# A split-precision SwiGLU layer on one core: both token halves share each weight tile, the gate-up product goes through memory, and the down projection sums over all channels in PSUM

## The reference, cut to what matters

```python
def _rmsnorm(x, g):
    xf = x.astype(jnp.float32)
    y = xf * lax.rsqrt(jnp.mean(xf * xf, axis=-1, keepdims=True) + EPS)
    return (y * g.astype(jnp.float32)).astype(x.dtype)
    ...
    h = _rmsnorm(x, g_fp)
    f = (jax.nn.silu(h @ w_g) * (h @ w_u)) @ w_d
    x = x + _rmsnorm(f, g_fq)
```

## Time and profile before

| | us |
|---|---|
| median of 3 runs | 1560.63 (1560.19 to 1563.69) |
| the profiled execution | 1561.2 |
| its span, first to last instruction | 1559.3 |
| PE busy | 1494.7 (96%) |
| DVE busy | 958.9 (61%) |
| ACT busy | 683.7 (44%) |
| POOL busy | 460.6 (30%) |
| TensorE clock granted, mean | 0.991 |

### The profile page before, as it was taken

The page is one execution under the profiler, slowest core; times in us unless marked ns, Lnnn a source line. Parts: engine busy times, 40 slices in busy tenths (PEclk is TensorE's granted clock), DMA queues, the critical chain, the costliest instruction groups (busy, mean ns, idle before and its releaser), DMA issues.

```text
span 1559.3 us, 27456 instructions
## 1 busy us (share of the span) xinstructions
PE 1494.7 (96%) x10941; PEld 1438.2 (92%) x10941; DVE 958.9 (61%) x1628; ACT 683.7 (44%) x1356; POOL 460.6 (30%) x392
## 2 busy tenths in 40 slices
PE   7999999999999999999889999999989999999998
PEld 7999999999999999986789989999989999999897
DVE  6105551343114364836887868879689788796976
ACT  6225543552225412446745525344355454444544
POOL 2000000000000133510673434647266445463541
PEclk9999999999999999999999999999999999999999
DMA  5111112001112143145523323233324332333332
GB/s 190 55 40 41 41 51 89 28 28 41 41 31 82 48 151 115 56 158 193 176 82 123 122 72 106 71 111 83 102 82 138 106 124 58 121 94 109 95 103 116
DMA packets 174599, 143.28 MB, mean 92 GB/s; under 512 B 6966, under 2 KB 149310, under 8 KB 174476
## 3 DMA queue, kind: packets, MB, share of 16 engines
q1 hardware_dynamic: 170584, 129.44, 27.1%
q0 software_dynamic: 2720, 7.89, 1.7%
q10 hardware_dynamic: 1172, 4.23, 0.7%
HBM read 129.59 MB, written 11.95 MB: 91 GB/s over the span
## 4 chain that ended last, share of the span: by engine, by line
PE 75%; DVE 15%; issue 4%; POOL 3%; DMA 2%; ACT 2%; DVEq 0%; SPq 0%; ACTq 0%; POOLq 0%
PE bank L718 9%; PE bank L720 9%; PE bank L719 9%; DVE s_lo L2286 8%; PE bankC L718 3%; PE bankC L720 3%; PE bankC L719 3%; PE psT L714 3%; PE psAB L1194 3%; PE psAB L1195 3%; PE psAB L1196 3%; PE bankC L1234 2%; PE bankC L1236 2%; PE bankC L1235 2%; PE bank L1236 2%
## 5 line engine op out<-in xcount | busy, mean ns | idle before, releaser
L2286 DVE TENSOR_TENSOR s_lo<-raw,s_hi 128x512 fp32r<-128x512 f32 x308 | 316.2, 1049 | 3.5 <-ACT s_hi L1704 3.5
L1704 ACT ACTIVATE s_hi<-raw 128x512 fp32r<-128x512 f32 x308 | 187.5, 625 | 158.5 <-PE bankC L1236 66.7
L718 PE MATMUL bank<-h_hi,w_hi 128*128 128x344 f32 x752 | 249.5, 332 | 3.3 <-DVE h_lo L1868 3.1
L720 PE MATMUL bank<-h_hi,w_lo 128*128 128x344 f32 x752 | 241.5, 321 | 0.0
L719 PE MATMUL bank<-h_lo,w_hi 128*128 128x344 f32 x752 | 241.4, 321 | 0.0
L1855 DVE TENSOR_TENSOR w_lo<-w_raw,w_hi 128x1024 fp32r<-128x1024 f32 x71 | 90.2, 1270 | 203.5 <-ACT w_hi L1309 141.7
L718 PEld LDWEIGHTS bank<-h_hi,w_hi 128*128 128x128 f32 x752 | 142.6, 190 | 7.6 <-POOL w_lo L2486 3.3
L2506 POOL MEMSET smask<- 32x24 f32 x1 | 0.1, 108 | 503.5 <-PE psT L925 503.5
L1194 PE MATMUL bank<-fop,s_hi 128*128 128x258 f32 x440 | 129.1, 293 | 18.7 <-DVE ev L2353 10.3
L719 PEld LDWEIGHTS bank<-h_lo,w_hi 128*128 128x128 f32 x752 | 142.5, 189 | 0.0
L720 PEld LDWEIGHTS bank<-h_hi,w_lo 128*128 128x128 f32 x752 | 142.4, 189 | 0.0
(11 more groups left out here) (505 smaller groups left out, 4328.5 us busy)
## 6 DMA issues: line engine op xcount, KB each, us to landing
raw<-in_w_gate SPq DMA_DIRECT2D x44, 512.0 KB, 4.0
raw<-in_w_up SPq DMA_DIRECT2D x44, 512.0 KB, 5.3
raw<-in_w_down SPq DMA_DIRECT2D x44, 512.0 KB, 4.4
w_raw<-in_w_in SPq DMA_DIRECT2D x42, 512.0 KB, 4.0
w_raw<-in_w_out SPq DMA_DIRECT2D x24, 512.0 KB, 3.7
xin<-in_x_prompt SPq DMA_DIRECT2D x8, 512.0 KB, 7.6
xr<-x_rows SPq DMA_DIRECT2D x8, 512.0 KB, 7.5
xn<-in_x_prompt SPq DMA_DIRECT2D x7, 512.0 KB, 4.5
```

Of the source, the lines that this page charges most:

```text
L718: mm(out[:, 0:TG], w_hi[par][:, ws], hi[:, k, tgc[tg]], start=first, stop=False)
L720: return mm(out[:, 0:TG], w_lo[par][:, ws], hi[:, k, tgc[tg]], start=False, stop=last)
L1704: fn(slot(q, 0), split_source(q), ACT.Copy).then_inc(sp_hi, 1)
L2286: v.tensor_tensor(slot(q, 1), split_source(q), slot(q, 0).bitcast(F32), ALU.subtract).then_inc(sp_lo, 1)
```

## The change

All of it is in the sub-layer. The text names the positions in the new order **jobs**.

- 26 jobs (`NJ`) replace 44 pairs. `HALVES` says which halves a job does: jobs 0 to 3 tile 0 to 3 for half 0 alone, jobs 4 to 21 their tile for both halves, jobs 22 to 25 tiles 0 to 3 again for half 1 alone. In a job for both, each block is done for half 0 and at once for half 1 with the same split weights; each half has its own three PSUM banks.
- The products of a job are put in `ab` and stored to a tensor in memory (`store`). After the stores of job 21 SP loads quarters 0 and 1 of it back (`a_load`: 6 DMAs each, rows of 1032 B), later quarters 2 and 3. `a_high` and `a_low` (now on DVE) split whole groups of up to 4 channel tiles.
- `down(n, c)`: 8 channel blocks for half 0, then 8 for half 1; each takes one block of 128 output channels and one quarter, and adds all 22 hidden tiles (66 matmuls) in one bank. ACT takes the result out, scaled by the gain, and its square (`copy_out`). POOL adds the squares (`add_square`). PE sums them over channels with a matmul against a column of ones (`z_sums`), and turns the tiles (`z_tile`); DVE scales and adds x (`z_final`).
- The chain of the last three token tiles runs in jobs 0 to 2, that of half 1's operands in jobs 2 to 4. S3 of the features is formed by DVE (`f_third`), low parts of the four plain blocks overwrite them, and four of the seven low parts are made by DVE.

The diff, cut to its core:

```diff
+NF = 22
+AHEAD = 4
+NJ = NF + AHEAD
+HALVES = [(0,)] * AHEAD + [(0, 1)] * (NF - AHEAD) + [(1,)] * AHEAD
...
@@ sync engine
+            def job_load(j):
+
+                if j >= 2:
+                    sp.wait_ge(sp_lo, 7 * (j - 1))
                 for e, w in enumerate((wg, wu)):
+                    sp.dma_start(w_pair(j)[:, e], chunks(w, 0, 8, P * tile_of(j), P)).then_inc(raw_in[j % 2], 16)
...
+            def store(j):
+                hs = HALVES[j]
+                cols = slice(2 * NQ * hs[0], 2 * NQ * hs[0] + 2 * NQ * len(hs))
+                sp.wait_ge(sum_s, summed(j, "prod0", hs[-1]))
+                sp.dma_start(a_d[tile_of(j)][:, cols], ab_of(j)[:, cols]).then_inc(a_out[j % 2], 16)
...
+            for j in range(2, NJ):
+                job_load(j)
+                store(j - 2)
...
+                if j == NF + 1:
+                    sp.wait_ge(pe_ev, event(NF - 1, 6, 0))
+                    for x in range(2):
+                        sp.wait_ge(a_out[x], 8 * NF)
...
+                    a_load(0)
+                    a_load(1)
+                if j == NF + 2:
+                    down_load(0)
+            store(NJ - 2)
+            down_load(1)
+            store(NJ - 1)
...
+            a_load(2)
...
@@ tensor engine
+            for j in range(NJ):
                 for o in range(7):
...
+                    if j == 2 and o in (1, 3, 5):
+                        f_turn(6 + o // 2)
+                    for h in HALVES[j]:
+                        block(j, o, h)
+            for n in range(16):
+                down(n, 0)
+                if n == 8:
+                    z_first_sums()
+                elif 9 <= n < 14:
+                    z_tile(Z_ORDER[n - 9])
+                down(n, 1)
...
@@ scalar engine
+            def job(j):
+
+                q, hs = 7 * j, HALVES[j]
                 high(q + 5)
+                for h in hs:
...
+                    fn(part(j, h, "p1"), banks(j, h)[0], ACT.Copy).then_inc(lu_s, 1)
+                if j == 0:
+                    y_root(2)
+                elif j == 1:
+                    x1_squares()
...
                 high(q + 6)
                 high(q + 7)
+                for h in hs:
...
+                    fn(part(j, h, "g1"), banks(j, h)[0], ACT.Silu).then_inc(lu_s, 1)
...
@@ vector engine
+            def job(j):
...
                 low(q + 4)
                 low(q + 5)
+                for h in hs:
...
+                    v.tensor_tensor(part(j, h, "u2"), y, part(j, h, "p1"), ALU.add).then_inc(sum_s, 1)
...
                 low(q + 6)
                 low(q + 7)
+                for h in hs:
...
+                    v.tensor_tensor(part(j, h, "u3"), y, part(j, h, "p1"), ALU.add).then_inc(sum_s, 1)
+                if j == 0:
+                    y_factor(2)
+                    x1_term(6)
+                elif j == 2:
+                    f_copy(7)
+                elif j == AHEAD - 1:
+                    f_third(1)
                 low(q + 8)
...
+                elif j > NF:
+                    a_low(0, 2 * (j - NF) - 2)
+                    a_low(0, 2 * (j - NF) - 1)
```

More of the change, by code:

```diff
@@ L143, in down_groups @@
[L143 to L154, removed]
+SLOTS = 6
+KG = [(4 * i, min(4, NF - 4 * i)) for i in range(6)]
+DOWN = 7 * NJ
+SPLITS = DOWN + 6 * 16
+EVENTS = 7 * PAIRS
+Z_ORDER = (0, 1, 2, 3, 8, 4, 5, 6, 7, 9)
@@ new lines, in z_root @@
+            def z_root(t):
+                n, rows = Z_ORDER.index(t), z_rows(t)
+                act.wait_ge(z_pe, Z_SUMMED[t])
+                fn(stat[0:rows, n:n + 1], z_sum(t), ACT.Sqrt, scale=1.0 / D, bias=stat[0:rows, 62:63]).then_inc(z_sd, 1)
+            for j in range(NJ):
+                job(j)
+            for n in range(16):
+                u = DOWN + 6 * n
+                high(u + 5)
+                if n:
+                    copy_out(n - 1, 1)
+                if n in (0, 8):
+                    for kg in range(6):
+                        a_high(1 if n == 0 else 3, kg)
+                copy_out(n, 0)
+                if n == 8:
+                    for t in Z_ORDER[:5]:
+                        z_root(t)
+                for kg in range(6):
+                    if n == 7:
+                        a_high(2, kg)
+                    if kg < 5:
+                        high(u + 6 + kg)
@@ L1840, in _ @@
+            z_root(4)
+            z_root(5)
+            copy_out(15, 1)
+            for t in (6, 7, 9):
                 z_root(t)
@@ L2320, in _ @@
                 if g == 2:
-                    f_low(0, 0)
+                    f_third(0)
                 lo_out(8 * g + 6)
@@ L2472, in _ @@
-            z_half(7, 1)
-            y_add(1, ROUNDS - 1, 15)
-            for t in (9, 4, 5):
-                z_last(t)
+                    v.scalar_tensor_tensor(cols, half[psZ[t]][a][0:rows, :], stat[0:rows, 10 + n:11 + n], cols, ALU.mult, ALU.add
+                                           ).then_inc(z_s, 1)
+            for j in range(NJ):
+                job(j)
+            for n in range(16):
+                u = DOWN + 6 * n
+                low(u + 4)
+                low(u + 5)
+                if n in (0, 8):
+                    for kg in range(6):
+                        a_low(1 if n == 0 else 3, kg)
+                if 9 <= n < 14:
+                    z_final(Z_ORDER[n - 9])
+                for kg in range(6):
+                    if n == 7:
+                        a_low(2, kg)
+                    if kg < 4:
+                        low(u + 6 + kg)
```

1061 lines of the change are left out of this document (489 added, 572 removed).

## The result

The changed kernel takes 1564.58 us (median of 20 runs, 1559.18 to 1566.85) beside 1559.57 for the kernel before (20 runs, 1555.16 to 1564.48). The ratio is 1.0027, 95% interval 1.0017 to 1.0037: slower by 0.27% (5.0 us by medians), where 1548.3 was forecast. The number is inside the range of 1532 to 1573; the direction is the other one. The profiled execution took 1565.85 us, its span 1564.1, 17.2 more than the 1546.9 of the forecast.

What follows compares the result with a forecast made beforehand. DVE and POOL were taken to bound the pairs, PE `down`. S3 of job 4 at 852 + 651.2 for 450 blocks + 10 + 24 = 1537.2, + 9.7 tail = 1546.9, or 1548.3 as median; range 1532 to 1573.

Steps and rivals of the forecast that it cites:

- S3 of job 4 at 852: End of the first five jobs: PE's block S3 of job 4 starts at 852 (846 to 860), 26.8 us lost before.
- the forecast's own sign of 20 to 35: First five jobs: the forecast is wrong if they lose less than 20 or more than 35 us.
- slow read-back: Rival at the join: loading 5.81 MB back takes longer than 18.7 us; above 1563.7 from 34 us on; chance 0.15.
- the double jobs don't run full: Rival in jobs 4 to 21: something holds each of 18 jobs 1.2 us, 22 us in all, giving 1570; chance 0.10.
- Work and double jobs: PE's work unchanged at 1.447 us a block; jobs 4 to 21, each for both halves, lose 0.
- Job 0: Start of the sub-layer: DVE's job 0 starts at 779.9 as before, p1 about 1 us later behind two feature splits.
- DVE's line from there to u2 of job 4: First jobs on DVE: 9.6 us a job, 18.2 for moved chains, 11 beside POOL, 3 for ACT.
- The join, 24 us: Between jobs and `down`: PE loses 24 us (14 to 40), 17.5 of it as tile 24's load queues behind the read-back.
- the queue doesn't hold `job_load(24)`: Rival at the join: that small load passes the twelve read-back loads, 19.5 of 24 us go, giving 1529; chance 0.13.
- `down`: 0: In `down`: DVE's six low parts at half 1's start fall 2.7 us behind with 7 us of lead; cost 0.
- The tail, 9.7: Behind the last matmul: 6.9 us to DVE's last step and 2.8 for the store, 9.7 in place of 14.25.
- the start chain is longer: Rival in jobs 0 to 3: ACT or the tile-to-tile chain costs 10 to 15 us more, 1558 to 1563; chance 0.12.

Runs made afterwards that it cites:

- e14_act0: e12_low0 with ACT making job 0's weight splits and the last two feature splits ahead of the last three tiles' squares: 1561.58 us, ratio 1.0009.
- e12_low0: Changed kernel with ACT's copy p1 of job 0 made early and half 0's three POOL low parts made by DVE: 1564.38 us, ratio 1.0026.
- e6_lows: Changed kernel with all seven low parts of half 1's features on DVE, the late four moved into job 4: 1560.20 us, ratio 0.9997.
- e5_sums: Changed kernel with half 1's three feature sums formed by DVE instead of POOL: 1563.44 us, ratio 1.0025.
- e11_wsums: Changed kernel with POOL's weight sums of tiles 1 to 4 cut to 8 of each 128 columns: 1558.77 us, ratio 0.9992.
- e3_light: Changed kernel with most scaling and adding of the last three token tiles and half 1's feature difference left out on DVE: 1558.98 us, ratio 0.9994.
- e1_order: Changed kernel with SP requesting weights of jobs 24 and 25 and the first down tile ahead of or between the two read-backs: 1546.75 us, ratio 0.9915.
- e4_gather: Changed kernel with DVE waiting, before quarter 3's low parts in `down`, until POOL has gathered the sample tokens' columns: 1559.78 us, ratio 0.999.

## Why the prediction was wrong, step by step

The step that failed is the first five jobs: S3 of job 4 at 852, with 26.8 us lost ahead of it. It started at 865.48, with 40.2 lost, outside the forecast's own sign of 20 to 35. A second one, smaller, is `down`, where the waits were put at 0 and cost about 5. Together they are more than the 12.4 us that were to be gained. The measured time is in the range by luck: above 1563 the range stood mostly for a slow read-back and for double jobs that are held, and neither came.

*Work and double jobs: right.* 1.441 us a block against 1.447, and no wait in the double jobs. That is 2.7 us less over 450 blocks. The rival "the double jobs don't run full" falls.

*S3 of job 4 at 852: wrong, it started at 865.5.* This is the largest miss, 13.3 us against the unrounded 852.2. It falls into three parts:

- *Job 0, 6.6 us.* The forecast has DVE begin at 779.9, so that u2 of job 0 ends at 781.6; it ended at 788.24. Its words were "p1 comes about 1 us later, two feature splits now stand ahead of it". p1 let PE go on 4.6 us later than before (784.15, 779.58). The changed `f_high` waits for the last `wo` matmul for four of its seven splits, so four splits of 1.06 us, the squares and the copies stood ahead of job 0's splits. The added wait in `f_high` wasn't priced. With ACT's order changed S3 of job 0 came 4.7 us earlier and the whole 3.0 (e14_act0, with DVE's low parts of e12_low0 in it; 4.0 and 2.8 against that run).
- *DVE's line from there to u2 of job 4, 2.5 us.* It took 73.1 us (788.24 to 861.38) where the forecast's terms, 9.6 a job, 18.2 of moved steps, 11 for POOL and 3 for ACT, make 70.6. So as a sum these terms were nearly right. The moved steps priced at 18.2 lasted 25.6 in the trace, 7.4 more, beside POOL. The count of POOL's steps was wrong: three low parts of half 1 are its own, two of them ahead of S3 of job 4 (851.67, 855.15), and not one.
- *The path, 4.1 us.* The forecast followed DVE to u2 of job 4 and let PE start S3 at once. But S2 of job 4's half 1 comes before S3, and it needs a low part of half 1 that DVE made at the end of job 3, in 4.53 us with its neighbour. PE stood for it until 858.80 and then had three blocks to do before S3, 6.7 us in place of 4.3, since the clock was 0.51 at first.

What each of these costs is worth when it is taken away, the runs say: POOL's low parts 3.9 us at S4 of job 4 (4.4 by median, e6_lows), its feature sums 3.1 (1.1 by median, e5_sums), its weight sums 7.5 (5.8, e11_wsums), 9 us of DVE's moved steps 7.1 (5.6, e3_light).

The clock was left out in the first jobs. The forecast had one row of a dip, 1.8 us, and used it at the join alone. Over 90 us from 780 the clock is 0.85, and right behind the long stops it is at 1.2 GHz (0.51 in the window from 858.80). Where the starts of matmuls lie further apart than 0.12 us, summed over the 9 us behind a stop, PE lost 3.1 us behind the stop of 7.15, 2.3 behind 6.28, 1.7 behind 4.50 and 2.3 behind 4.63, but 0.1 behind 2.61 (848.15). Part of this is hidden where DVE is the bound.

Behind S3 of job 4 there was 1.39 more, at its S4, where POOL's weight sums of tile 5 stood behind its last low part.

*The join, 24 us: right, and so was its mechanism.* PE stopped at T+17.8 (T = 1221.0, the end of job 21) and job 23's S4 started at T+36.0, with T+18 and T+37.1 forecast; `down` began at T+64.2, with T+64.5 forecast (28 blocks and 24 us). The loads ran at 354 GB/s, 16.4 us for 5.81 MB and inside the bounds of 14 and 22, and SP's queue was held 13.70 us by the issue of twelve DMAs. The rival "the queue doesn't hold `job_load(24)`" falls: with the queue's order alone changed the stop is gone (e1_order). The rival "slow read-back" falls too. Whether rows that start off a boundary of 256 B cost anything, no run here shows, since none has the same loads on the boundary; at 354 GB/s nothing depended on it.

*`down`: 0 was wrong by about 5.* The forecast said that DVE's lead hides its six low parts, which it does for PE. It didn't ask who else is held by them: POOL's copy lasted 8.23 us, PE waited 2.39 and lost some at low clock. `down` took 269.4 us for 264.7 forecast; e4_gather gave back 4.8 by median and 5.6 in `down`.

*The tail, 9.7: right.* From the last matmul of `down` to the end of the span:

```profile
1554.69 0.28 PE L1277 MATMUL bank<-a_hi,s_lo 128*128 128x258 f32 x1
```
```profile
1560.58 1.40 DVE L2480 SCALAR_TENSOR_TENSOR xd<-bankC,stat,xd 4x512 f32<-4x512 f32 x2
```

1554.8 to 1564.1 is 9.3, where before it was 14.25.

*The sum of the misses* against the last matmul at 1537.2: 13.5 (S3 of job 4 at 865.5; the slow clock ahead of it is in this) - 0.4 (from there to the end of job 21: 355.6 us for 356.0, the wait of 1.39 against the better pace) - 0.3 (join) + 4.7 (`down`) = 17.5, as found (1554.7).

The rival that came true is "the start chain is longer", given 0.12, with 10 to 15 us and 1558 to 1563. Its place was right and its mechanism half: not the tile-to-tile chain became the bound, but DVE beside POOL and ACT's order.

## What to carry to other kernels

When work is moved into a place where the engines already wait for each other, count its steps on every engine from the code, and price each by the row that has it beside the other engine, not alone. A big read-back that is queued ahead of a small load that the next step needs costs the whole of its issue: put the small one ahead of it, which was worth 17.8 us here. Follow every operand that PE needs in its own order, not only the sum that it waited for before. And add to a long stop of PE what the clock takes behind it, here 1.7 to 3.1 us behind stops of 4.5 us and more, and 2.6 behind one of 2.39.

## What the hardware showed that was not expected

- A POOL copy of 16 elements a partition took 8.23 us where DVE ran two-input steps back to back, 1.91 where DVE was held for it, 0.20 where DVE was idle. The small instruction wasn't favoured.
- A DVE low part of 128x1032 took 1.23 us alone, 2.3 to 3.4 beside POOL; two of 128x512 took 1.28 and 3.4 to 4.6.
- SP was held for 13.70 us by the issue of twelve DMAs (ten of 516 KB and two of 258), and 6.00 by six, while a single load ahead of them was issued in 0.37 to 0.59 us (e1_order); rows of 1032 B were moved at 354 GB/s.
- The granted clock behind a stop of the same length isn't the same in every execution: 0.89 and 0.83 over the same 30 us with stops of 2.39 and 2.38 us in them, and `down` is 267.9 to 270.8 us long with that stop. Where the stop of 2.4 us was gone (e4_gather) the clock was 1.00.
